# State space mixer: the four squared tiles of a gated group added up by GpSimd, and one TensorE product per group for the sum over rows

## What is computed

```
y = y_diag + y_off + d_skip * x
y = y.reshape(bsz, T, SSD_D_INNER) * silu(z)
yg = y.reshape(bsz, T, G, SSD_D_INNER // G)          # G = 8 groups of 512
yg = yg * rsqrt(mean(square(yg), -1) + RMS_EPS)
y = yg.reshape(bsz, T, SSD_D_INNER) * norm_w
return y @ w_out
```

## Time and profile before

| | |
|---|---|
| median of 3 runs | 3564.98 us (3558.92, 3564.98 and one of 10472.52) |
| profiled execution, own time | 3563.67 us |
| its span, first to last instruction | 3561.7 us |
| mean granted TensorE clock | 0.973 of full |
| busy: PE / DVE / ACT / POOL | 94% / 62% / 52% / 12% |
| the SSD input projection | from about 1390 to 1917 us of the span |

### The profile page before, as it was taken

The page is one execution under the profiler, slowest core; times in us unless marked ns, Lnnn a source line. Parts: engine busy times, 40 slices in busy tenths (PEclk is TensorE's granted clock), DMA queues, the critical chain, the costliest instruction groups (busy, mean ns, idle before and its releaser), DMA issues.

```text
span 3561.7 us, 59815 instructions
## 1 busy us (share of the span) xinstructions
PE 3358.5 (94%) x25261; PEld 3084.7 (87%) x25261; DVE 2214.6 (62%) x2919; ACT 1842.9 (52%) x2890; POOL 435.5 (12%) x594
## 2 busy tenths in 40 slices
PE   7899999999899998999999989999989999899798
PEld 2688888878689998999999989999989889888797
DVE  1787767432655455666766475555576556899756
ACT  1444434232567646676775354555455554767444
POOL 0011111001000000000000010000010002788301
PEclk9999999999999999999999999999999999899899
DMA  9655556622234554555554545555544345333354
GB/s 389 227 200 167 187 189 222 215 84 100 83 124 143 173 181 158 185 175 190 178 178 161 184 147 180 170 167 168 174 145 163 128 135 173 119 129 125 105 180 146
DMA packets 158106, 591.89 MB, mean 166 GB/s; under 512 B 18368, under 2 KB 18400, under 8 KB 156048
## 3 DMA queue, kind: packets, MB, share of 16 engines
q1 hardware_dynamic: 135072, 495.54, 41.4%
q0 software_dynamic: 22192, 90.44, 7.5%
q10 hardware_dynamic: 576, 2.10, 0.2%
HBM read 585.79 MB, written 2.21 MB: 165 GB/s over the span
## 4 chain that ended last, share of the span: by engine, by line
PE 63%; DVE 12%; PEld 10%; DMA 6%; ACT 6%; issue 3%; POOL 0%; PEldq 0%; SPq 0%; DVEq 0%; ACTq 0%; POOLq 0%
PE psum_all L513 18%; PE psum_all L517 18%; PE psum_all L515 18%; DMA raw<-in_stream 4%; PEld psum_all L517 3%; PEld psum_all L513 3%; PEld psum_all L515 3%; DVE w_lo L459 2%; DMA mod_early<-in_stream 2%; ACT w_hi L452 1%; DVE s_vd L2923 1%; PE psum_all L1344 1%; PE psum_all L1314 1%; ACT ssd_seg L1883 1%; DVE s_vb L2922 1%
## 5 line engine op out<-in xcount | busy, mean ns | idle before, releaser
L513 PE MATMUL psum_all<-act_hi,w_hi 128*128 128x256 f32 (+1 forms) x6704 | 2052.0, 306 | 72.7 <-DVE act_lo L895 45.8
L515 PE MATMUL psum_all<-act_lo,w_hi 128*128 128x256 f32 (+1 forms) x6704 | 2019.8, 301 | 0.0
L517 PE MATMUL psum_all<-act_hi,w_lo 128*128 128x256 f32 (+1 forms) x6704 | 2018.8, 301 | 0.0
L459 DVE TENSOR_TENSOR w_lo<-raw,w_hi 128x1024 fp32r<-128x1024 f32 x866 | 1075.7, 1253 | 980.0 <-ACT w_hi L452 978.8
L513 PEld LDWEIGHTS psum_all<-act_hi,w_hi 128*128 128x128 f32 x6704 | 1295.1, 193 | 134.0 <-issue 71.9
L452 ACT ACTIVATE w_hi<-raw 128x1024 fp32r<-128x1024 f32 x866 | 910.1, 1057 | 913.4 <-DMA raw<-in_stream 910.1
L515 PEld LDWEIGHTS psum_all<-act_lo,w_hi 128*128 128x128 f32 x6704 | 1295.8, 193 | 43.9 <-issue 3.1
L517 PEld LDWEIGHTS psum_all<-act_hi,w_lo 128*128 128x128 f32 x6704 | 1294.6, 193 | 41.5
L746 DVE SCALAR_TENSOR_TENSOR xT<-mod_late,small,xT 128x1024 f32<-128x1024 f32 x210 | 256.4, 1280 | 3.9 <-DMA mod_late<-in_stream 1.5
L706 POOL DMA_DIRECT2D mod_late<-in_stream x128 | 68.0, 532 | 587.3 <-DVE xT L746 435.6
L972 POOL TENSOR_TENSOR ln_acc<-xT 128x256 f32<-128x256 f32 x8 | 5.9, 738 | 1017.9 <-DVE xT L1709 1017.9
(11 more groups left out here) (472 smaller groups left out, 3343.5 us busy)
## 6 DMA issues: line engine op xcount, KB each, us to landing
raw<-in_stream SPq DMA_DIRECT2D x866, 512.0 KB, 3.3
mod_late<-in_stream POOLq DMA_DIRECT2D x128, 512.0 KB, 4.5
mod_early<-in_stream SPq DMA_DIRECT2D x64, 512.0 KB, 8.9
ssd_seg<-acs_rows POOLq DMA_DIRECT2D x8, 1536.0 KB, 6.8
xT<-in_x SPq DMA_DIRECT2D x1, 2048.0 KB, 16.1
ctxT<-in_ctx SPq DMA_DIRECT2D x1, 2048.0 KB, 20.4
ctxT<-in_ctx POOLq DMA_DIRECT2D x1, 2048.0 KB, 9.4
xT<-in_x POOLq DMA_DIRECT2D x1, 2048.0 KB, 8.1
```

Of the source, the lines that this page charges most:

```text
L459: dve.tensor_tensor(w_lo[:, n % RING, :], raw[:, n % RING, :], w_hi[:, n % RING, :].bitcast(F32), ALU.subtract).then_inc(lo_ready, 1)
L513: pe.matmul(sums, w_hi[:, n % RING, cols], block.rhs(kk, True, block.width), start=(kk == 0), stop=False)
L515: pe.matmul(sums, w_hi[:, n % RING, cols], block.rhs(kk, False, block.width), start=False, stop=False)
L517: last = pe.matmul(sums, w_lo[:, n % RING, cols], block.rhs(kk, True, block.width), start=False, stop=(kk == block.kt - 1))
```

## The change

Instead of four products per group, accumulated in PSUM, there is one. GpSimd first adds the four squares of the group in place: tiles 2 and 3 on tiles 0 and 1 (one instruction of 128x512), then tile 1 on tile 0 (128x256). TensorE multiplies tile 0 alone by `over_512`. The product stands in the slot in which the group's last product stood.

```diff
-            gated, squared, summed = (signal("ssd_" + n, 4 * G) for n in ("gated", "squared", "summed"))
+            gated, squared = (signal("ssd_" + n, 4 * G) for n in ("gated", "squared"))
+            summed, sq_added = signal("ssd_summed", G), signal("ln_added", 2 * G)
...
-            gate_at, square_at, sum_at = z_slots(1, n_in), z_slots(2, n_in), z_slots(2, n_in)
+            gate_at, square_at, sum_at = z_slots(1, n_in), z_slots(2, n_in), slots_of(last_z, 2)
...
-                for k in sum_at.get(slot, ()):
-                    pe.wait_ge(squared.sem, squared.at(k + 1))
-                    if k and k % 4 == 0:
-                        pe.wait_ge(rooted.sem, rooted.at(k // 4))
-                    pe.matmul(psum[7][:, 0:T], const("over_512"), sq[:, k % 4, :], start=(k % 4 == 0), stop=(k % 4 == 3)) \
+                for g in sum_at.get(slot, ()):
+                    pe.wait_ge(sq_added.sem, sq_added.at(2 * g + 2))
+                    if g:
+                        pe.wait_ge(rooted.sem, rooted.at(g))
+                    pe.matmul(psum[7][:, 0:T], const("over_512"), sq[:, 0, :], start=True, stop=True) \
                       .then_inc(summed.sem, 1)
...
-                    act.wait_ge(summed.sem, summed.at(4 * g + 4))
+                    act.wait_ge(summed.sem, summed.at(g + 1))
...
-                        act.wait_ge(summed.sem, summed.at(k - 3))
+                        act.wait_ge(summed.sem, summed.at(k // 4))
...
+                    if g >= 2:
+                        add_squares(pool, g - 2)
+                add_squares(pool, G - 2)
+                add_squares(pool, G - 1)
+
+            def add_squares(pool, g):
+                pool.wait_ge(squared.sem, squared.at(4 * g + 4))
+                pool.tensor_tensor(sq[:, 0:2, :], sq[:, 0:2, :], sq[:, 2:4, :], ALU.add).then_inc(sq_added.sem, 1)
+                pool.wait_ge(sq_added.sem, sq_added.at(2 * g + 1))
+                pool.tensor_tensor(sq[:, 0, :], sq[:, 0, :], sq[:, 1, :], ALU.add).then_inc(sq_added.sem, 1)
```

## The result

The changed kernel takes **3580.2 us** (median of 8 runs, 3574.43 to 3589.66), the kernel before 3565.89 us (8 runs, one of them of 10472.52 us; 3564.98 us without it). The ratio is **1.0050, 95% interval 1.0039 to 1.0060**: half a percent slower, well inside 2%. The profiled execution of the changed kernel took 3580.09 us with a span of 3578.2 us, 16.5 us more than before.

A forecast was written before the change was run, and what follows sets the result against it. TensorE, busy for 94% of the span, was taken to bound the kernel. On the profiled 3563.7 us: -10.3 - 2.1 + 24.4 + 9.8 = +21.8, that is 3585 us; range 3561 to 3597.

The forecast's parts named there:

- 24 products, -10.3 us: TensorE's queue at the sum product: 24 of 32 products go at 0.43 us each, 10.3 us saved.
- 2.1 us of old waits: TensorE's idle time for squares at the sum product's line, replaced by the new waits: 2.1 us more saved.
- The new wait, 24.4 us: TensorE at the remaining product waits for GpSimd's two additions behind the last square: eight stalls, together 24.4 us.
- Blocked, not free: GpSimd's additions wait for VectorE's two-SBUF-operand instruction: stalls 24.4 us, not 17.2; rival, free additions or clock that holds: 0.2.
- The clock, +9.8 us: TensorE's granted clock falls to 0.50 behind seven stalls above 2.17 us, 1.4 us each: 9.8 us.
- Nothing given back: Later waits of TensorE, such as those at L1835, stay near 16.6 us and return nothing: 0.
- swallowed: Rival: the waits at L1835, 16.6 us in all, shrink by the new stalls; 3550 to 3565 us, chance 0.12.
- The rival with VectorE's delay: Late taps and w_lo reach TensorE, another 1 to 1.5 us per group: 3593 to 3599 us, chance 0.11.
- The clock came back: Against the rival that a stall leaves the clock at 0.50 for much of the group: over 3640 us, chance 0.02.

The follow-up runs named there:

- e1: Changed kernel without any additions, one product per group on the fourth tile's square alone: ratio 0.9969 to the kernel before, stage 545.8 us.
- e6: Changed kernel with the product a slot later in groups 0 to 5, GpSimd's additions there held until VectorE's third w_lo behind the square: ratio 1.0021.
- e3: Changed kernel with five useless products of constants ahead of each group's waiting product, filling TensorE's stall: ratio 1.0029 to the kernel before.
- e2: Kernel before with its 32 products, each group's last also waiting for two GpSimd additions into an unread spare tile: ratio 1.0083.
- e9: Changed kernel with a third dependent GpSimd addition of 128x256 behind the two, which the product also waits for: ratio 1.0107 to the kernel before.
- e12: e7 without any GpSimd addition, the mean square leaving out tiles 1 and 2 (group 7: tile 1): ratio 0.9984 to the kernel before.
- e7: Changed kernel with GpSimd adding only early tiles 1 and 2 on tile 0, TensorE making two products per group (three in group 7): ratio 0.9985.
- e10: e7 timed again, the same kernel: ratio 0.9972 to the kernel before, stage 552.0 us.

## Why the prediction was right

The forecast was 3585 us, +21.8 on the profiled execution; it was +16.4 (3580.09 against 3563.67), and the median 3580.2. The sign, the mechanism and the size of the whole hold; that it came so near is partly luck, since the clock was put 3 us too high, what comes back was put at nothing, and single stalls missed by -0.3 to +0.9 us. The forecast also held 2% to be about what a measurement of this kernel can tell; the interval of 0.1% on either side shows that it tells far less. Taken step by step:

- **24 products, -10.3 us, and 2.1 us of old waits.** Right in sum: e1 has -11 us by its ratio and -12.2 in the stage. The 2.1 us are the weak part. Of them 1.7 us were idle time of TensorE's weight loading and 0.4 of its multiplying, and e1, where the same waits for squares were left, had 3.6; other waits became shorter instead.
- **The new wait, 24.4 us.** Right: 25.2 us. The parts: the first addition 1.99 to 2.07 us where the sum had 2.0; from there to the end of the second 0.87 where the sum had 1.1, since the tap that I let go first was over 0.28 us behind the first addition and not 0.5; in groups 1, 2 and 5 above all the square came later against the moment TensorE was ready than in the trace of before, by which those stalls came out longer (3.0, 3.2 and 4.1 us for 2.7, 2.9 and 3.2), and in groups 3 and 4 they were shorter than forecast (2.6 and 3.1 for 2.9 and 3.3). In group 7 the order was as forecast (3.5 us for 3.8).
- **Blocked, not free.** Right, and shown by e6: 1.29 us with VectorE idle, 1.99 with it in L459. The rule of the Trainium skill ("SBUF — State Buffer", section "SBUF: two separate sides"), an exclusive lock held for a whole instruction, fits e6's additions and its `w_lo`. The forecast took the 16 additions of L2997, free though VectorE seemed busy, as speaking against a lock. Read one by one they speak for it: beside 14 of them stands a VectorE instruction that began earlier, took 2.2 to 5.6 us where the same line takes 0.4 to 1.2 elsewhere, and ended behind the addition, so it was VectorE that was held; the one that began inside a running L459 took 2.08 us. One of the 14, whose VectorE instruction takes 0.68 us elsewhere (trace of before):

```profile
3109.64 2.57 DVE L2932 TENSOR_TENSOR s_im_c<-s_vd,s_cos 128x512 f32<-128x512 f32 x1
3110.35 1.31 POOL L2997 TENSOR_TENSOR s_frac<-s_frac,s_turn 128x512 f32<-128x512 f32 x1
```

- **The clock, +9.8 us.** That idle time costs clock is right (e3: filling it gives 7.5 us back); the size was off, and so was the way to tell which stalls bring a fall. The sum had seven falls of 1.4 us, put down to every stall over 2.17 us. There were six, with two of them twice as long (groups 4 and 5); none behind 3.0 us in group 1 and 2.6 us in group 3, and one behind 2.1 us in group 6. That six came near seven is luck: e2 has much the same stalls, and only those of groups 0, 3 and 7 were followed by the lower clock, with four falls at the turning of `x`. And of the four falls at the turning of `x` three did not come again, though the wait of 2.73 us in group 4 was as long as those that had brought one. The stage's time at 0.50 is 31 us in the changed kernel and 14 before; 2.1 of those 17 us lie inside the stalls of groups 4 and 5 and cost nothing; of the rest 12 products lost per 3.2 us make some 6.5 to 7 us.
- **Nothing given back.** I took 0 for what later waits return; it was 1.0 us at the turning of `x`, 1.8 at `cb` (4.3 to 2.5 us) and 0.9 for `w_lo` (1.2 to 0.3).

In sum: -12.4 + 25.2 + 6.5 to 7 - 3.7 = +15.6 to +16.1, where the two spans differ by 16.5 us and the two stages by 17.5. The rival "swallowed" is refuted by e1, e2 and e9: the waits at the turning of `x` stayed between 15.6 and 17.0 us in them and the changed kernel. The rival with VectorE's delay is refuted by the waits for `w_lo`, which did not grow in the stage (1.2 us before and 0.3 after), and by e12, which is no faster than e7 and e10. The clock came back within 7 us in every case.

## What to carry to other kernels

A product spared on the busiest engine is worth its 0.43 us only if its replacement is not the last thing that this engine waits for: look at how late the last input comes (here 0 to 1.2 us of room) before putting a chain of 3 us behind it. Split such a sum so that the helper works on the inputs that are early and the busy engine takes the last one itself; that kept 15 of the 24 savings and no wait for GpSimd. A helper that arrives while VectorE is in an instruction like `w_lo` should be costed at its blocked duration (here 1.99 us for 1.29), and a stall on TensorE at more than its length: in the changed kernel 25.2 us of stalls brought 6.5 to 7 us of lower clock with them.

## What the hardware showed that I had not expected

- Idle time alone did not tell whether the granted clock fell: it fell behind 1.92 us of idling in group 6 of the changed kernel and held behind 2.85 us in group 1 and 2.73 us at the turning of `x` in group 4. Which stall brings a fall these runs do not tell:

```profile
1560.15 0.48 PE L1817 MATMUL psum_all<-ssd_sq,consts 128*128 128x256 f32 x1 [2.85 <-POOL ssd_sq L2035]
...
1669.40 0.44 PE L1836 MATMUL psum_all<-consts,ssd_x 128*128 128x128 f32 x2 [2.73 <-ACT ssd_x L1875]
...
1909.56 0.51 PE L1817 MATMUL psum_all<-ssd_sq,consts 128*128 128x256 f32 x1 [1.92 <-POOL ssd_sq L2035]
```

- Useless products ahead of a wait made the kernel faster than the same kernel without them, by 7.5 us of 3580, 2 to 13 us by the intervals (e3).
- VectorE adds 128x512 in 0.68 us and 128x256 in 0.42; GpSimd takes 1.29 and 0.73 undisturbed, and 1.99 for the 128x512 one behind a running `w_lo`.
